# Gated embedding: the casts of the weight slabs put behind earlier gates

## The reference

```python
def rms_norm(x, g):
    xf = x.astype(jnp.float32)
    y = xf * lax.rsqrt(jnp.mean(xf * xf, axis=-1, keepdims=True) + EPS)
    return (y * g.astype(jnp.float32)).astype(x.dtype)

for layer in range(DEPTH):          # DEPTH = 2
    ...
    h = h + 0.5 * swiglu(rms_norm(h, ffn2_g[layer]), ffn2_wg[layer], ffn2_wu[layer], ffn2_wd[layer])
    gate = jax.nn.sigmoid(rms_norm(h, ple_g[layer]) @ ple_wgate[layer])
    h = h + gate * (p[layer] @ ple_wproj[layer])
```

## Time and profile before

| what | before |
|---|---|
| median of three executions | 3197.04 us |
| the profiled execution, whole time | 3198.65 us |
| its span, first to last instruction | 3197.3 us |
| mean granted TensorE clock | 0.987 of full |
| TensorE matmuls busy | 3068.3 us, 96% |
| VectorE busy | 1316.1 us, 41% |
| ScalarE busy | 1186.7 us, 37% |
| GpSimd busy | 1104.5 us, 35% |

### The profile page before, as it was taken

How to read it: one execution, slowest core, us unless ns; L and a number is a source line. 1 busy time by engine, 2 the same in 40 slices (tenths; PEclk the granted TensorE clock), 3 DMA queues, 4 the chain that set the end, 5 groups by cost and what they waited for, 6 DMA issues and landing times.

```text
span 3197.3 us, 36195 instructions
## 1 busy us (share of the span) xinstructions
PE 3068.3 (96%) x14292; PEld 2474.5 (77%) x14292; DVE 1316.1 (41%) x2377; ACT 1186.7 (37%) x2090; POOL 1104.5 (35%) x463
## 2 busy tenths in 40 slices
PE   8999998799999999999989999989999999999998
PEld 6888777578888878887758888877768878866787
DVE  5311396624121361121874231185544252256532
ACT  3222375643232442223424332253332342355432
POOL 4444442014444444444004444423424423300143
PEclk9999999899999999999999999999999999999999
DMA  4233232013233223233313233323313325300032
GB/s 145 93 99 99 80 126 66 1 34 102 96 99 96 91 91 98 93 99 92 96 40 118 93 99 96 95 92 103 98 58 93 94 89 184 126 7 1 28 99 73
DMA packets 78187, 278.27 MB, mean 87 GB/s; under 512 B 8599, under 2 KB 9495, under 8 KB 77636
## 3 DMA queue, kind: packets, MB, share of 16 engines
q1 hardware_dynamic: 78020, 275.96, 27.5%
HBM read 273.78 MB, written 6.08 MB: 88 GB/s over the span
## 4 chain that ended last, share of the span: by engine, by line
PE 84%; DVE 11%; ACT 3%; issue 2%; POOL 1%; DMA 0%; DVEq 0%; SPq 0%; ACTq 0%; POOLq 0%
PE ps L486 24%; PE ps L488 24%; PE ps L487 24%; PE ps L1568 3%; PE ps L1542 2%; DVE arena L2425 1%; DVE arena L1824 1%; PE ps L1554 1%; PE ps L3120 1%; PE ps L2475 1%; DVE w_lo L471 1%; DVE arena L1904 1%; DVE arena L1903 1%; PE ps L2916 1%; POOL w_lo L461 1%
## 5 line engine op out<-in xcount | busy, mean ns | idle before, releaser
L461 POOL TENSOR_TENSOR w_lo<-ring,w_hi 128x1024 fp32r<-128x1024 f32 x447 | 1089.9, 2440 | 1961.1 <-ACT w_hi L438 1919.7
L486 PE MATMUL ps<-x_hi,w_hi 128*128 128x512 f32 x2168 | 857.4, 395 | 34.3 <-POOL w_lo L461 21.2
L488 PE MATMUL ps<-x_hi,w_lo 128*128 128x512 f32 x2168 | 847.1, 391 | 0.0
L487 PE MATMUL ps<-x_lo,w_hi 128*128 128x512 f32 x2168 | 847.0, 391 | 0.0
L438 ACT CAST w_hi<-ring 128x1024 fp32r<-128x1024 f32 x473 | 493.8, 1046 | 723.6 <-PE ps L488 714.5
L486 PEld LDWEIGHTS ps<-x_hi,w_hi 128*128 128x128 f32 x2168 | 409.0, 189 | 127.0 <-issue 19.6
L487 PEld LDWEIGHTS ps<-x_lo,w_hi 128*128 128x128 f32 x2168 | 409.1, 189 | 88.0 <-issue 4.1
L488 PEld LDWEIGHTS ps<-x_hi,w_lo 128*128 128x128 f32 x2168 | 408.9, 189 | 86.4
L486 PE MATMUL ps<-r_hi,w_hi 128*128 128x512 f32 x1120 | 436.1, 389 | 0.0
L488 PE MATMUL ps<-r_hi,w_lo 128*128 128x512 f32 x1120 | 435.7, 389 | 0.0
L487 PE MATMUL ps<-r_lo,w_hi 128*128 128x512 f32 x1120 | 435.7, 389 | 0.0
(11 more groups left out here) (265 smaller groups left out, 3330.0 us busy)
## 6 DMA issues: line engine op xcount, KB each, us to landing
ring<-in_stream SPq DMA_DIRECT2D x473, 512.0 KB, 3.5
arena<-in_cmp_w SPq DMA_DIRECT2D x16, 512.0 KB, 3.7
frev_copies<-frev SPq DMA_DIRECT2D x16, 240.0 KB
arena<-frev_copies SPq DMA_DIRECT2D x1, 3072.0 KB, 12.9
h<-in_x SPq DMA_DIRECT2D x4, 512.0 KB, 7.7
out<-arena SPq DMA_DIRECT2D x4, 512.0 KB
arena<-in_p SPq DMA_DIRECT2D x2, 512.0 KB
arena<-in_mem SPq DMA_DIRECT2D x1, 1024.0 KB
```

The source lines that it names most:

```text
L461: self.nc.gpsimd.tensor_tensor(self.w_lo[:, n % SPLIT, :], self.ring[:, n % RING, :], self.w_hi[:, n % SPLIT, :].bitcast(F32), ALU.subtrac ...
L486: nc.tensor.matmul(out, a[0], b[0], start=start, stop=False)
L487: nc.tensor.matmul(out, a[0], b[1], start=False, stop=False)
L488: return nc.tensor.matmul(out, a[1], b[0], start=False, stop=stop)
```

## The change

`k.high` is called with an entry of a table of eight in place of m + 1. All other code stays as it is, and so does the set of casts.

```diff
+    ahead = (4, 5, 5, 6, 6, 7, 8, 8)
+
     with Stage(nc) as block:
...
                 act.wait_ge(scaled.handle, scaled.at(m + 1))
                 nc.scalar.activation(buf[:, m % 4, :], buf[:, m % 4, :], ACT.Sigmoid).then_inc(gate.handle, 1)
-                k.high(act, first + m + 1 + SPLIT)
+                k.high(act, first + ahead[m] + SPLIT)
                 if fed and 1 <= m <= fed.spare:
                     fed.round(act, m - 1)
                 if not fed and m >= 1:
```

## The result

| what | before | after |
|---|---|---|
| median of 20 executions each, us | 3197.09 | 3201.1 |
| lowest and highest, us | 3195.8 to 3198.87 | 3199.05 to 3206.68 |
| the profiled execution, whole time and span, us | 3198.65, 3197.3 | 3205.35, 3204.0 |
| mean granted TensorE clock | 0.987 | 0.985 |

The ratio is 1.0014, with a 95% interval of 1.0008 to 1.0021. In the bounds of the prediction that is no change; the interval lies wholly above 1, so there is a real loss, of about 4 us (2.6 to 6.7 by the interval).

A forecast was written before the change was run, and what follows sets the result against it. It took the chain of gates, not the slab wait, to bound the end of each part. Layer 0's chain 1.82, clock 0 and layer 1 0.4 gave +2.2 us on 3197.04: 3199.3 us, range 3193.5 to 3202.5.

The forecast's parts named there:

- The bound: Both layers' gated embeddings: the gate chain, not the slab, decides when TensorE goes on; the removed 3.07 us wait comes back.
- rival 1: TensorE's pace sets the end of a part, so removed waits are passed on as gain: 3187.5 us, chance 0.07.
- The chain of A: Layer 0's gated embedding: line 1477 of gate 7, and TensorE's restart for the next stage, come 1.82 us later.
- The chain of B: Layer 1's gated embedding: line 1477 of gate 7 comes 0.45 us later, counted from gate 1.
- The clock in A: Half rate behind TensorE's restart after layer 0's gated embedding: difference taken as 0, bounds -1.7 to +1.7 us.
- The end of B: Root behind layer 1's gated embedding, and everything hanging on it: +0.4 us, bounds -0.4 to +1.6.
- full rate, the squares late: End of layer 1's gated embedding: the product before the total runs at full rate; the root moves by -0.4 us.
- The sum: Whole kernel: 1.82 + 0 + 0.4 = +2.2 us, median 3199.3 us, chance 0.60.
- Rival 2: Meetings fall otherwise: GpSimd starts over 1.7 us after slab 7's cast, so line 748 goes first; 3194.7 us, chance 0.13.
- Rival 3: TensorE's clock stays at half rate longer after the joined gaps in both layers: +7.7 us, 3204.7 us, chance 0.10.
- Rival 4: No net effect, gains and losses of the gate chain cancelling: 3197.0 us, chance 0.10.

The follow-up runs named there:

- e8: Round or square ahead of the cast, plus a separate table per layer chosen so subtractions meet few VectorE operations, against the change: 3190.89 us, ratio 0.998.
- e3: The change with slab 7 cast behind gate 2 instead of gate 1, so ScalarE does not stand for product 4: 3197.74 us, ratio 1.0004.
- e4: The change with the round (layer 0) or square (layer 1) ahead of the cast on ScalarE: 3195.64 us, ratio 0.9996.
- e6: The change plus useless TensorE matmuls (34 in layer 0, 32 in layer 1) filling the wait before the next stage: 3197.82 us, ratio 1.0001.
- e1: The change's table in layer 0 only, the old order in layer 1: 3199.04 us, ratio 1.0008.
- e11: The unaltered change measured once more against the kernel before: 3200.86 us, ratio 1.0013.
- e2: The change's table in layer 1 only, the old order in layer 0: 3197.55 us, ratio 1.0004.
- e5: The kernel before, old table, with only the round or square moved ahead of the cast: 3194.64 us, ratio 0.9991.
- e7: The kernel before plus useless TensorE matmuls (13 in layer 0, 12 in layer 1) in its waits: 3198.25 us, ratio 1.0004.
- e9: e8 plus useless TensorE matmuls (12 in layer 0, 8 in layer 1) in the remaining waits: 3189.92 us, ratio 0.9976.
- e10: The change's form, cast first, with other tables per layer that put two casts behind one gate: 3193.08 us, ratio 0.9985.

## Why the prediction was right, and where it was off

**The bound.** Right. The wait of 3.07 us before product 6 went, and the time did not follow: it came back in front of the next stage as the 3.55 and 4.53 us above, forecast as 3.5 and 4.9. With rival 1 (3187.5 us) the time would have fallen with the wait; it rose. e8 shortened the gates, with the same work on TensorE, and took 6 us away.

**The chain of A.** Forecast +1.82, measured +1.85. Gate 1 to 2 was forecast as 7.35 and is 7.37; gate 4's meeting is gone as forecast. The whole path from the earlier trace rows held: the end of product 4, cast, 1.11 us, subtraction, 0.55 us. e3 takes the stall away and leaves a meeting with line 748; e4 takes that meeting away, and there ScalarE's stand for product 4 (1.40 us) delays no gate, since the round is ahead of it.

**The chain of B.** Forecast +0.45 from gate 1 to 7, measured +0.47. The steps inside it were less exact: gate 1 to 2 is 3.53 us, and the cost fell on the interval to gate 3 (5.29); I had put the intervals as 2.72, 6.07 and 5.59 to gate 4, and they are 3.53, 5.29 and 5.65; to gate 3 that is 8.79 forecast and 8.82 measured. In B I had left out that slab 6's subtraction meets line 1485 of gate 1 (1.50 us in place of 0.69); it cost nothing in the sum, since gate 2 stands behind slab 7's cast anyway.

**The clock in A.** The term that was mis-sized. I took 0, since the half rate would follow a restart as before; it did, but for 5.2 us in place of 3.4, +0.9 (within my bound of 1.7). e6 shows what half rate costs behind this restart: 2.4 us of A. The trace of before held one restart of this kind in A, and I took its length for a constant.

**The end of B.** Forecast +0.4 of bounds -0.4 to +1.6; the root came at -0.5, a tenth beyond the bound. The product before the total ran at full rate (2140.43 to the total at 2143.97 is 3.54 us, where it was 5.60), so it is the case that I had called "full rate, the squares late", and its figure of -0.4 was good. What I had no term for is the half rate some 24 us further on, 1.6 us. Whether the change causes it stays open. TensorE has a wait of 2.27 us, from start to start, ahead of that place in all thirteen traces (both kernels and e1 to e11). In nine of them the half rate follows: in every run with the change's table in part B (after, e2, e4, e6, e11), and in e5, e7, e8 and e9. In four it doesn't: the kernel before, e1, e3 and e10.

**The sum.** Forecast +2.2; the stretches give +2.73 and +1.16, 3.9. Of the 1.7 that are missing 0.9 are the clock in A, 1.6 the late half rate in B, less 0.9 for the root. The median of 3201.1 lies 1.8 above the forecast of 3199.3. That it is so near is in part luck, since in B two errors of opposite sign stand against each other.

**The rivals.** Rival 2 was wrong: GpSimd followed slab 7's cast by 1.12 us, not 1.7, and VectorE did not come first. Rival 3 was partly right: in A the joined gaps are followed by more half rate, 0.9 us' worth. In B the 6.8 us at half rate around the joined gap are as many as the two stretches of 3.4 were before, and it is open whether the late 1.6 belong to it; even with them it is 2.5, below the 4.2 from which it would have decided. The Trainium skill (TensorE: Matmul & The Clock Gate, section "Why this matters for your kernels") asks for short gaps; the trace agrees in A, where the longer gap cost more, and e9's 0.84 us cost nothing. But gaps of nearly one length fell on both sides here (before product 6 of part A, 3.46 us and in e2 3.52 left the clock at 1.00, and 3.49 in e7 did not), so no row of this case gives a border. Rival 4 was wrong: both chains grew, and the interval lies above 1.

**Chain and clock together.** Take from the kernel before its 1.7 us at half rate: A is then 51.27 with 26.06 of gates. Add the change of the gates and half of the time at half rate behind the restart, and every run's A but one comes out:

| kernel | gates, change | at half rate behind the restart | A worked out | A measured |
|---|---|---|---|---|
| after | +1.85 | 5.2 | 55.72 | 55.70 |
| e11 | +1.82 | 5.2 | 55.69 | 55.64 |
| e1 | +1.78 | 5.6 | 55.85 | 55.81 |
| e2 | -0.02 | 3.4 | 52.95 | 52.97 |
| e3 | +0.81 | 3.0 | 53.58 | 53.62 |
| e4 | -1.47 | 5.4 | 52.50 | 52.47 |
| e5 | -0.73 | 0 | 50.54 | 50.65 |
| e6 | +1.93 | 0 | 53.20 | 53.30 |
| e8 | -3.49 | 3.4 | 49.48 | 49.51 |
| e9 | -3.47 | 0 | 47.80 | 47.89 |
| e10 | -2.54 | 3.1 | 50.28 | 50.30 |

Only e7 lies outside (51.29 worked out, 52.47 measured), by the 1.19 us for which its filling ran over. So part A needs no third term above a tenth of a us.

Part B comes out as well, from 461.16 us, the change of its root (counted from the total ahead of it, 45.57 us in the kernel before) and 1.6 us where the late half rate follows:

| kernel | root, change | late half rate | B worked out | B measured |
|---|---|---|---|---|
| after | -0.48 | yes | 462.28 | 462.32 |
| e11 | -0.50 | yes | 462.26 | 462.23 |
| e1 | +0.02 | no | 461.18 | 461.20 |
| e2 | -0.50 | yes | 462.26 | 462.28 |
| e3 | -0.12 | no | 461.04 | 461.07 |
| e4 | -1.65 | yes | 461.11 | 461.17 |
| e5 | -3.69 | yes | 459.07 | 459.13 |
| e6 | -0.39 | yes | 462.37 | 462.37 |
| e7 | -0.60 | yes | 462.16 | 462.16 |
| e8 | -4.73 | yes | 458.03 | 458.06 |
| e9 | -4.69 | yes | 458.07 | 458.12 |
| e10 | -3.10 | no | 458.06 | 458.09 |

This table takes the root as measured; it shows that behind the root nothing but that half rate makes the runs differ.

## What to carry to other kernels

Before moving an operation out of one engine's way, list which operations of the other engines it will lie beside in its new place, and add up the meetings gate by gate: here that replay gave every chain's length within 0.7 us, most within 0.2, while the wait that was removed told nothing. Where a VectorE operation with two SBUF inputs and a GpSimd subtraction must meet, let the VectorE operation start first (e4), or put two subtractions in a row: in e10 the two cost 3.0 us together, against 2.1 for a single one that meets line 748 in the kernel before (5.47 in place of 3.38). What the clock adds, 0 to 2.8 us behind one restart, varies by as much as such an edit brings, so compare by stretches between fixed points and not by one execution's span.

## What the runs showed of the hardware

- A VectorE operation with two SBUF inputs that starts during GpSimd's subtraction is held and ends 0.55 us behind it. In the kernel after all 27 operations of lines 748, 1485, 1486 and 625 that start so do this, among them the line 748 shown above (1133.78 against 1133.23); so do line 748 in e3 (1131.06 against 1130.52) and line 1485 in e4 (1128.77 against 1128.22). I had expected a fixed price for a meeting; it is what is left of the subtraction, so the operation lasts 2.65 us or 1.71 or 1.86. Four traces (e7 to e10) have one exception each, right behind three runs of line 748: in e8 the subtraction's row begins at 1146.35 while line 748 still runs, line 1485 begins at 1146.56 and takes its plain 0.69 us, and the subtraction lasts 3.12. It had been passed.
- It holds the other way too, hidden in the duration. The subtraction in e4 that starts while no such VectorE operation runs shows 2.40 us; those that start under one show 2.63 in the earlier trace rows and 2.64 to 2.83 in e4. The Trainium skill (SBUF — State Buffer, section "Who interferes with whom") says that who issues first holds the ports that VectorE and GpSimd share for the whole instruction; the rows agree with that in both directions, but for the four exceptions above.
- Waits from start to start: 3.46 us left the granted clock at 1.00 in the kernel before, 3.52 in e2 too, and 3.49 us in the same place was followed by 0.50 in e7. In part B of the kernel before 0.50 followed 2.79 us (2.52 in brackets), in e10 2.80 us there left it at 1.00. Later in part B one wait of 2.27 us was followed by 0.50 in nine traces and not in four. How long the half rate lasts behind a restart isn't set by the gap alone either: behind 5.03 to 5.05 us from start to start it was 5.2 to 5.6 us in the kernel after, e1, e4 and e11, and 3.0 in e3; behind 3.0 to 3.4 us it was 3.1 to 3.4 in the kernel before, e8 and e10.
